# Output projection begun inside the heads' loop, and the opening done block 0 first, in a four-layer transformer kernel on one core

## What is computed

```python
h = modulate(rmsnorm(x, norm_g[layer, 0]), sh1, sc1)
x = x + 0.5 * g1 * swiglu_2(h, ffn_w1[layer, 0], ffn_w3[layer, 0], ffn_w2[layer, 0])
h = modulate(rmsnorm(x, norm_g[layer, 1]), sh2, sc2)
proj = h @ w_in[layer]
...
oa = moba_attention(qa, ka, heads(va, N_HEADS_A))
ob = dsa_attention(qb, kb, heads(vb, N_HEADS_B), qi, ki, wi)
oc = stick_breaking_attention(heads(qc, N_HEADS_C), heads(kc, N_HEADS_C), heads(vc, N_HEADS_C))
o = jnp.concatenate([oa, ob, oc], axis=2)
o = (_rms(o).reshape(B, S, D_MIX) * out_g[layer].astype(jnp.float32)).astype(x.dtype)
x = x + g2 * (o @ w_out[layer])
h = modulate(rmsnorm(x, norm_g[layer, 2]), sh3, sc3)
x = x + 0.5 * g3 * swiglu_2(h, ffn_w1[layer, 1], ffn_w3[layer, 1], ffn_w2[layer, 1])
```

## Time and profile before

| | |
|---|---|
| median of 3 runs | 2866.26 us (2862.58, 2866.26, 2869.65) |
| the profiled execution | 2863.47 us, its span 2861.5 us |
| busy: PE, PEld | 2776.1 us (97%), 2427.2 us (85%) |
| busy: DVE, ACT, POOL | 1972.8 us (69%), 1371.5 us (48%), 228.7 us (8%) |
| mean granted TensorE clock | 0.993 of full |
| chain that ended last | PE 78%, DVE 14%, ACT 3%, POOL 2% |
| DMA | 564.43 MB, mean 197 GB/s |

### The profile page before, as it was taken

One profiled execution on the slowest core, in us unless ns is written; L12 is line 12 of the kernel. 1 busy time (PEld: TensorE's weight loads), 2 busy tenths in 40 slices (PEclk: granted clock), 3 DMA queues, 4 the chain that ended last, 5 costly groups with the idle time before them and its releaser, 6 DMA issues.

```text
span 2861.5 us, 37686 instructions
## 1 busy us (share of the span) xinstructions
PE 2776.1 (97%) x16040; PEld 2427.2 (85%) x16040; DVE 1972.8 (69%) x2217; ACT 1371.5 (48%) x1554; POOL 228.7 (8%) x201
## 2 busy tenths in 40 slices
PE   7999999999999999999999998999999999999999
PEld 6889999998888889999998887878878878787787
DVE  6768876655666678876555666676876676778644
ACT  4544545455444445545454444444644444446433
POOL 0000420000000000520000000003000000030000
PEclk9999999999999999999999999999999999999999
DMA  8664433445776655333446676653257676442453
GB/s 297 249 223 183 155 120 131 156 171 197 272 265 237 255 206 189 137 141 125 169 156 231 257 258 234 258 219 133 89 222 256 250 266 255 177 147 87 181 189 147
DMA packets 82039, 564.43 MB, mean 197 GB/s; under 512 B 9072, under 2 KB 10576, under 8 KB 15952
## 3 DMA queue, kind: packets, MB, share of 16 engines
q1 hardware_dynamic: 66272, 465.47, 44.5%
q0 software_dynamic: 15600, 96.55, 9.0%
HBM read 560.86 MB, written 1.12 MB: 196 GB/s over the span
## 4 chain that ended last, share of the span: by engine, by line
PE 78%; DVE 14%; ACT 3%; POOL 2%; issue 2%; DMA 1%; SPq 0%; DVEq 0%; POOLq 0%; ACTq 0%
PE ps L332 72%; DVE ring_lo L327 4%; ACT w_hi L320 2%; PE ps L881 1%; POOL qk L2006 1%; PE ps L1269 1%; POOL rope_a L2002 1%; DMA rows<-mod_rows 1%; PE ps L513 1%; DVE h_lo L559 1%; DVE a_hg L1789 1%; DVE e L518 0%; PE ps L1397 0%; PE ps L1423 0%; DVE e L975 0%
## 5 line engine op out<-in xcount | busy, mean ns | idle before, releaser
L327 DVE TENSOR_TENSOR ring_lo<-ring,w_hi 128x2048 fp32r<-128x2048 f32 x422 | 972.9, 2308 | 498.6 <-ACT w_hi L320 487.5
L320 ACT ACTIVATE w_hi<-ring 128x2048 fp32r<-128x2048 f32 x422 | 806.4, 1911 | 331.2 <-PE ps L332 201.4
L332 PE MATMUL ps<-w_hi,h_hi 128*128 128x512 f32 (+1 forms) x1920 | 729.5, 380 | 15.9 <-DVE h_lo L559 11.7
L332 PE MATMUL ps<-w_hi,h_lo 128*128 128x512 f32 (+1 forms) x1920 | 717.0, 373 | 0.0
L332 PE MATMUL ps<-ring_lo,h_hi 128*128 128x512 f32 (+1 forms) x1920 | 716.3, 373 | 0.0
L332 PEld LDWEIGHTS ps<-w_hi,h_hi 128*128 128x128 f32 x1920 | 363.9, 190 | 83.6 <-issue 13.2
L332 PE MATMUL ps<-h_hi,w_hi 128*128 128x256 f32 x1488 | 430.9, 290 | 1.3 <-DVE h_lo L559 1.3
L332 PE MATMUL ps<-h_lo,w_hi 128*128 128x256 f32 x1488 | 422.3, 284 | 0.0
L332 PE MATMUL ps<-h_hi,ring_lo 128*128 128x256 f32 x1488 | 422.2, 284 | 0.0
L332 PEld LDWEIGHTS ps<-w_hi,h_lo 128*128 128x128 f32 x1920 | 363.5, 189 | 64.7
L332 PEld LDWEIGHTS ps<-ring_lo,h_hi 128*128 128x128 f32 x1920 | 364.3, 190 | 61.2 <-issue 1.4
(11 more groups left out here) (343 smaller groups left out, 3447.8 us busy)
## 6 DMA issues: line engine op xcount, KB each, us to landing
ring<-stream SPq DMA_DIRECT2D x438, 1024.0 KB, 4.8
e<-ada POOLq DMA_DIRECT2D x77, 1024.0 KB, 5.8
rows<-mod_rows POOLq DMA_DIRECT2D x18, 512.0 KB, 5.4
rows<-gain_rows POOLq DMA_DIRECT2D x8, 512.0 KB, 4.4
val<-c_row POOLq DMA_DIRECT2D x4, 512.0 KB, 5.0
x<-x_in SPq DMA_DIRECT2D x4, 256.0 KB, 6.7
mem<-mem_t SPq DMA_DIRECT2D x1, 1024.0 KB, 16.7
out_t<-x SPq DMA_DIRECT2D x4, 256.0 KB, 2.1
```

Source lines behind the costliest of these rows:

```text
L320: nc.scalar.activation(hi_of(p), ring[:, p % RING, :], ACT.Copy).then_inc(S.w_hi_ready, 1)
L327: nc.vector.tensor_tensor(lo_of(p), ring[:, p % RING, :], hi_of(p).bitcast(F32), ALU.subtract).then_inc(S.w_lo_ready, 1)
L332: mm = nc.tensor.matmul(out, a, b, start=start and n == 0, stop=stop and n == 2, skip_group_check=group)
```

## The change

Three places change.

1. In the heads' loop of the second block, four of the sixteen parts (block 0, both column halves, pairs 0 and 1) are issued inside the last three turns instead of behind the loop: two at the head of turn 8, one at the head of turn 9, one at the head of turn 10. Each waits for its pair's `o_ready` (and the first of each column for its weight tile and for its bank to be read). Behind the loop, only block 1's four parts of these pairs remain.
2. In the opening, ACT and DVE do block 0 of `x` before weight tile 0, and on ACT block 1's squares go before `high` of tile 2.
3. At the end, the last two quarters are each multiplied and added one after the other, where before both were multiplied first.

```diff
+        def first_act(act):
+
+            square(act, 0, 0, x_loaded[0])
+            square(act, 0, 1, x_loaded[1])
+            h_high(act, 0, 0, 4)
+            h_high(act, 0, 1, 4)
+            high(act, 0)
+            high(act, 1)
+            ln_table()
+            rstd_act(act, 0, 0)
+            square(act, 0, 2, x_loaded[2])
+            square(act, 0, 3, x_loaded[3])
+            high(act, 2)
+            h_high(act, 0, 2, 4)
+            h_high(act, 0, 3, 4)
+            rstd_act(act, 0, 1)
...
@@ first_late_dve
             into(0)
             into(1)
-            variance(dve, 0, 0)
             h_low(dve, 0, 0, 4)
             h_low(dve, 0, 1, 4)
+            low(dve, 0)
+            variance(dve, 0, 0)
             into(2)
             into(3)
...
@@ one_act
             if l == 0:
-                high(act, FFN_A)
-                late_act(act, 0, FFN_A + 1 - HIGHS, x_loaded)
+                first_act(act)
...
@@ one_dve
             if l == 0:
-                low(dve, FFN_A)
                 first_late_dve(dve, chain)
...
@@ two_pe
+            def out_first(c, pair):
+
+                pe.wait_ge(S.o_ready, nth(S.o_ready, pair + 1))
+                if pair == 0:
+                    pe.wait_ge(S.w_lo_ready, Z_O + c + 1)
+                    pe.wait_ge(S.zm_ready, nth(S.zm_ready, HEADS_2 - 1 + c))
+                out_part(c, 0, 0, pair)
...
                 if i in (0, 2):
                     tile(13 + i // 2)
+                if i == HEADS_2:
+                    out_first(0, 0)
+                    out_first(1, 0)
+                if i == HEADS_2 + 1:
+                    out_first(0, 1)
+                if i == HEADS_2 + 2:
+                    out_first(1, 1)
                 if 0 <= i - 1 < HEADS_2:
                     flip(i - 1)
                     sums(i - 1)
...
             for c in range(2):
-                pe.wait_ge(S.w_lo_ready, Z_O + c + 1)
                 for pair in range(2):
-                    pe.wait_ge(S.o_ready, nth(S.o_ready, pair + 1))
-                    for b in range(2):
-                        mm = out_part(c, 0, b, pair)
+                    mm = out_part(c, 0, 1, pair)
                 mm.then_inc(S.tile_done, 1)
...
@@ two_dve
                 plus(dve, 0)
                 plus(dve, 1)
-                gate_pair(dve, chain, 2, 4, ready)
-                plus(dve, 2)
-                plus(dve, 3)
+                for q in (2, 3):
+                    ready(q)
+                    chain(nc.vector.tensor_tensor(part_of(xs, q), ps[:, 4 + q, :], row_of(ROW_GATE, q), ALU.mult))
+                    plus(dve, q)
```

More of the change, by code:

```diff
@@ L407, in ln_table, with late_act @@
             nc.scalar.preload_act_table_set("natural_log_exp_and_others")
-        def late_act(act, n, p, ready=None):
+        def first_act(act):
[13 more added lines that the diff above has]
+            rstd_act(act, 0, 1)
+        def late_act(act, n, p):
             def sq(q):
-                square(act, n, q, ready and ready[q])
+                square(act, n, q)
             sq(0)
@@ L2287, in pair_sums, with out_part @@
                                  start=True, stop=True).then_inc(S.o_ss, 1)
+            def out_part(c, half, b, pair):
+                at = 2 * half + pair
+                for i, k in enumerate((at, 4 + at)):
+                    w = (2 * pair + i) * 512
+                    mm = triple(ps[:, 2 * b + c, :], both(h2, k, b * P, (b + 1) * P),
+                                weights(Z_O + 2 * half + c, w, w + 512), half == 0 and pair == 0 and i == 0,
+                                half == 1 and pair == 1 and i == 1)
+                return mm
+            def out_first(c, pair):
[4 more added lines that the diff above has]
+                out_part(c, 0, 0, pair)
             scores(0)
```

## The result

The changed kernel is slower: 2868.43 us in the median of 20 runs (2865.93 to 2870.94), against 2864.09 for the kernel before in its 20 runs beside them (2860.97 to 2869.79). The ratio is 1.0014, with an interval of 1.0007 to 1.002: 2 to 6 us lost (4.0 by the ratio, 4.3 by the medians), where 4.9 gained was forecast. The profiled execution took 2868.09 us.

What follows compares the result with a forecast made beforehand. The prediction took the kernel as mostly a queue of matmuls, with time to win only where TensorE waits. Opening 3.2, loop 1.15 and end 0.6 made 4.95, say 4.9 us, giving 2861 us, own range 2858 to 2864.

Steps and rivals of the forecast that it cites:

- The opening: Program start: with block 0 of x ahead of weight tile 0, the first matmul comes 3.2 us earlier, at about 14.6.
- The reading of the clock that was chosen: Opening: the slow clock ends a time after work begins, so the whole 3.2 us stays.
- the one instant: Opening: the slow clock ends at the same instant, 24.0, so the 3.2 us gained are worth 1.6.
- the term that the forecast put at nothing: Opening: tile 2's high part stands behind two more squares; taken as nothing, up to 1 us if late.
- The end: Program end: quarter 2's addition runs while DVE waits for TensorE, leaving one behind the last product; 0.6 us gained.
- The loop's term: Heads' loop, second block: four moved parts gain 0.75 us in one layer and 0.4 in the other, 1.15 together.
- still covered: End of heads' loop: pair_sums(3), ending at 2647.1, is ready before DVE takes it up at 2647.4.
- I leave the sum as it is: Behind the loop: tile Z_O + 4's load landing late, up to 1 us per layer, was not subtracted.
- the new hole on `ring_lo`: Projection behind the loop: TensorE stops about 2.1 us after five parts, waiting for low of tile Z_O + 3.
- rival C: Projection: the new hole drops the clock for the 18 matmuls behind it; 3.3 us slower, 2869; chance 0.12.
- Rival A: Opening and loop: clock rises at the same instant, DVE's chain is pushed; 0 to 1.2 us gained, 2865; chance 0.18.
- Rival D: Loop's end: DVE or ACT, not TensorE, holds it; loop 0, 3.8 us gained, 2862; counted within the forecast's 0.6.

Runs made afterwards that it cites:

- e1: Changed kernel with the heads' loop and projection as before, so only the opening and the end are changed: 2861.55 us, 0.9987 of the kernel before.
- e2: Kernel before with only the loop's and projection's part of the change (four parts moved): 2872.29 us, 1.0027 of the kernel before.
- e5: Changed kernel with POOL's c_row load, second block's first layer, held until tile Z_O + 4's high part is made: 2865.34 us, 1.0001 of the kernel before.
- e4: Changed kernel with a wait meant to hold POOL's c_row load that held nothing, in effect a repeat: 2867.74 us, 1.0008 of the kernel before.
- e6: Changed kernel with six matmuls that do no work ahead of the turning of block 0: 2865.39 us, 1.0003 of the kernel before.
- e8: Changed kernel with only two parts moved, one each at the heads of turns 9 and 10: 2861.2 us, 0.9983 of the kernel before.
- e7: Changed kernel with only turn 8's two parts moved: 2861.62 us, 0.9988 of the kernel before.
- e3: Changed kernel with only pair 0's two parts moved, between turn 9's two weigh and ahead of the last pair_sums: 2859.08 us, 0.9976 of the kernel before.
- e10: Changed kernel with two parts in TensorE's holes, a third ahead of the last pair_sums, and c_row held: 2857.64 us, 0.9974 of the kernel before.

## Why the prediction was wrong

**The opening was right.** 3.2 was forecast. In the ten traces that have it, the change's among them, the `low` of the fourth tile comes 2.8 to 3.8 us earlier than in the kernel before, and e1 gives the opening and the end together 3.7. The reading of the clock that was chosen, a time after work begins, came closer than the one instant: full rate came 3.5 us after the first matmul in the kernel after, at 18.3, and 6.1 in the kernel before, at 23.9. This is read from the distance of the matmuls, 0.43 us and then 0.23; the column of the granted clock reads 1.00 all through the opening in both. There is some luck in the number. The earlier full rate should have added to the 3.2, but where it came early TensorE met tile 2's `low` unfinished (0.42 us of waiting in the kernel after, 0.56 in e1), the term that the forecast put at nothing, and this took part of it back. The Trainium skill, "TensorE: Matmul & The Clock Gate", Part 1, has the slow start as a budget of time that differs from run to run; the traces agree that it differs (3.1 to 6.1 us over the ten kernels with the new opening). The rates of the earlier trace rows alone would not have told this.

**The end was right**, 0.6, by its rows.

**The loop's term was wrong, and it is the whole error**: +1.15 forecast, -7.7 measured (e2, interval 5 to 10). Three steps of it failed.

1. "DVE took that up at 2646.61 and does so at 2647.4 now: still covered." It was not. `pair_var(2)` was late by 1.1 and 0.8 us, as forecast (9.7 against 8.7 and 8.9 us after turn 7's `flip`). But DVE waited 0.64 for `pair_sums(3)`, and `pair_var(3)` was 1.8 and 1.6 late. The forecast has 6.0 us from one `pair_sums` to the next (2640.0 to 2646.0); it is 2084.07 - 2077.12 = 6.95, with TensorE busy all the way. The moved parts were priced at 0.227 a matmul, 5.45 for the four; in the chain they take 2.95 + 1.59 + 1.61 = 6.15. The last two, which lie between the two `pair_sums`, are 0.5 of the 0.95; the rest is in `pair_sums` and the matmuls of `weigh`, which take 3.75 there where the forecast leaves 3.27. With the distances of the forecast this step alone makes 5.85 - 4.3 - 1.8 = -0.25 and about 0 in the two layers: the gain is gone, and no more.
2. "I leave the sum as it is, because DVE isn't free for that tile's `low` before 2655.9." This is the largest. The Trainium skill's page "Trainium Kernel Development and Optimization", Key Constraints, has transfers of SP and POOL share the 16 DMA engines; the traces agree: 7.2 us for the tile that is waited for, against 5.0 for the same load before, and 6.3 with one of POOL's loads held back (e5). The page was cited, priced at 1 us per layer and then left out. Two things were missed besides. The `low` of that tile stands ahead of the gate product on DVE's list, so what is late there delays the norm at once. And with block 0's parts gone from behind the loop, tiles Z_O and Z_O + 1 are used up 2.7 us apart and not 5.4, so that two tiles of 1 MB load side by side with POOL's rows. Counted from turn 7's `flip` the rows begin 4.0 and 3.7 us later than before, but the tile's load only 1.1 and 0.9 later (19.4 against 18.3 and 18.5), so the two come closer together; the forecast had that load start as before. That `low` starts 2.9 us later in layer 1 and 1.6 in layer 2, and the first `h_low` of the next norm 2.3 and 1.1 later. e5 took away one of the transfers and gave back 0.9 in layer 1 (27.9 in the table, where the change, e2, e4 and e6 have 28.8 to 29.3). How the rest divides between the rows, the second tile and DVE's late chain wasn't separated.
3. "Against: before and behind this hole TensorE is busy without a break." True of the new hole on `ring_lo`, after which the clock stood. But rival C's mechanism came at the next place: ahead of the norm's turning TensorE now waits 1.86 and 0.83 us, where it arrived without a wait before, and behind the turning comes the 1.36 that was always there. The clock fell at that pair of holes, for 6.8 and 3.4 us, and cost 3.0 by the traces (e6). The fall of layer 1 came for 6.8 us in all three traces of this order (the change, e2, e4); that of layer 2 came in two of them. No size of hole that brings it can be read from these runs: 1.31 ahead of the turning brought none in e8, and 1.14 brought one in e7. The prediction asked of each new wait whether the clock would fall at it, and not of the old ones that a late release would lengthen.

Sum over both layers, from the table: 3.4 us are lost up to the first `h_low` (steps 1 and 2) and 2.7 from there to the sixth `low` (step 3). Of the 7.7 of e2 that leaves 1.6. The trace of e2 loses 1.2 between the two stretches of the table; the granted clock falls there in every trace, near 2492 in that of the kernel before, and the low stretch is 6.8 us long in the kernel before and 10.2 in e2 and in the change. In e3, without their late chain, it is 10.2 as well, so this is put down to the difference between one execution and another and not to the change.

Rival C had the right sign and nearly the right time, 2869, with 0.12; its place was wrong. Rival A had DVE's chain "pushed by nearly their whole length", and that wasn't so: 1.6 to 1.8 of 2.73. Rival D, in which something other than TensorE holds the end, is what happened, but its price of 0 was too kind, since a release that changes hands also moves what follows it.

What stays open: whether four parts in other places of the loop would do. The runs only show that two placed in the holes gain about 3 us (e3 against e1), that two at turn 8 or one each at turns 9 and 10 do no harm (e7, e8), and that a third adds nothing (e10). It is open too how the 3.4 us up to the first `h_low` divide between steps 1 and 2, and what decides whether the clock falls at a hole.

## What to carry to other kernels

When work is moved ahead of a wait, look first at what would end the wait then: go through the list of the waiting engine (here one `low` ahead of the gate product) and give every transfer that it hangs on a price of its own, including that buffers freed closer together load side by side. A hole in an engine's list is room only as long as its end doesn't hang on the work that is pushed; fill it between the instructions where it lies, and with as much as fits, then measure one part at a time, since here two parts gained, three did no more, and four lost all of it. And every lengthened idle stretch of TensorE, not only a new one, is a candidate for a lower clock in what follows it; look for it in more than one execution, since the same order of work had it in one and not in another (layer 2 of the change and of e4).

## What the runs showed of the hardware

- The clock fell to 1.2 GHz at two short holes around eight short turnings (1.86 and 1.36 us, first layer of the kernel after), though TensorE had worked for 9.8 us without a pause before them. With 1.5 us of matmuls that do no work, put ahead of the turning, the trace of e6 has 2.4 GHz in both layers, and they cost nothing measurable, because they stood in the wait. Holes of 1.31 and 1.36 us in e8 brought no fall.
- One and the same opening brought full rate 3.1 to 6.1 us after the first matmul in ten traces, yet the opening's worth stayed between 2.8 and 3.8 us.
- A load of 1 MB took 5.0 us with its follower 5.4 us behind and POOL's 2 MB begun 7.6 us ahead, and 7.2 to 7.7 with 2.7 behind and 4.7 ahead; with 1.5 MB on POOL and the same distances, 4.8 and 5.7 to 6.6.
